# Two attention layers whose units run in pairs on both halves of PE's rows and columns, with the output rows begun by token half

## The chip, the cores and the metric

The kernel runs on one core of a Trainium2 chip. The metric is the device time of one execution in microseconds (us). Three executions before the change took 1319.76, 1322.01 and 1323.81 us; the median is 1322.01 us.

## The reference

Two transformer blocks run one after the other on one sequence of 256 tokens and 1024 features, all in float32. The first block has two layers. Each is a mixer (attention) with an output projection, and a SwiGLU feed-forward. The second block has a feed-forward, a mixer of short convolution and state-space scan, and another feed-forward. The change touches the two attentions of the first block and what follows them directly:

```
mixer_ab: q (8 heads x 64), three branches on the same heads
  compressed keys (15), selected keys, window keys, each gated; then 8 more heads with sinks
mixer_cd: 8 softmax heads (causal over 256 tokens), 8 "stick-breaking" heads
each softmax head:   s = q @ k.T * 0.125 + bias(distance);  p = softmax(s);  o = p @ v
y = concat(o) @ w_out          # 1024 x 1024, the output rows
x = x + gate * rms_norm(y, w)
```

With 256 tokens every selection takes all blocks, so selected and window attention are dense and causal.

## The kernel before

One program is written out by hand for five engines, each in its own function (`pe`, `act`, `dve`, `pool`, `sp`), and all walk the same list of weight chunks (`stream_plan`). A chunk is 1 MB; SP loads it into one of five `raw` buffers. A weight half (128x1024) is split in two: ACT writes the rounded part into `HI`, DVE the remainder into `LO` (L1281), in six slots (`HL`), and PE multiplies by both (three matmuls for one product). A modulation chunk is used by DVE alone, in one fused product and sum (L1271). Every engine calls the same planner (`Walk`): `weight` brings the stream up to a half, `catch_up(n, ahead)` goes further, and `spare(n)` takes up to n modulation halves only.

The attention is cut into **units**. A unit is one query tile (`qt`, 128 tokens) of one branch and of either four heads on 128 keys (qt 0) or two heads on 256 keys (qt 1); both are 128x512 scores, one PSUM bank. Heads 0 to 3 lie on partitions 0 to 63 of the query tiles `FMT`, heads 4 to 7 on 64 to 127 (`hs`), so a score matmul uses 64 of PE's rows. The values matmul uses all rows and 64 of PE's columns; its half is that of the output's partitions (`o_ap`). `AB` has 18 units (selected, window and sink branch, six each), `CD` has 6. The accumulators of the attention output lie in PSUM banks 0 to 3; four banks more are work banks, taken and given in turn (`Banks`).

A unit goes through the engines like this: `scores` (PE), `biased` (DVE: scale and bias in one pass, L1443, the row maximum in a second, L1449 or L1457, and its negation), `exps` (ACT, one exponential per head, with its sum), `scaled` (DVE: 1/sum, gate, product, L1432), `transposes` (PE, four 128x128, L585), `moved` (ACT, copy out of PSUM), `values` (PE). `attend` runs one unit per step on each engine; on PE a step is

```
scores(tag, i, *U_[i])
if i > 1:
    transposes(tag, i - 2)
banks.give(("s", tag, i))
walk.spare(spare)
if between:
    between(i)
if i > 2:
    values(tag, i - 3, *U_[i - 3])
```

`between` weaves other work into the steps: in the first attention the compressed branch (`cmp_keys`, `cmp_values`, `cmp_scores`, `cmp_turn`, `cmp_out`, on DVE also `cmp_windows`), in the second the stick-breaking heads (`two_stages`). Three score slots and three slots for transposed scores (`s_slot`, `p_slot`) hold the units in flight.

After the last unit, `out_parts` copies each accumulator bank as `HH` (ACT) and `HLo` (DVE, L1348), `linear_out` runs the 8 contraction tiles of the output rows (`rows`: 12 matmuls of 128x512 per tile, both token halves one after the other; before the first, PE waits for the last `HLo`), `add_normed` adds the result to `x`, and `modulate` prepares the input of the feed-forward.

## Time and profile before

| | us |
|---|---|
| median of the executions | 1322.01 |
| the profiled execution | 1324.44 |
| its span | 1322.6 |
| mean granted TensorE clock, share of full | 0.963 |
| first attention: first score matmul to the end of the last values | 112.2 to 204.3 |
| its output rows | 209.2 to 232.2 |
| second attention | 506.7 to 550.4 |
| its output rows | 553.6 to 577.3 |

Times count from the span's start. PE stands for TensorE's matmuls, DVE for VectorE, ACT for ScalarE. A float32 matmul or transpose is counted as two instructions where both operands are plain float32. The end of a matmul is modelled and overlaps the start of the next, so that in a row "x8" the distance to the next row's start is the time that counts.

### The profile page before, as it was taken

The page shows a single profiled execution, that of the slowest core. Times are in us where ns is not written, and L with a number is a line of the kernel's source. Part 1 is how long each engine was busy: PE and PEld are TensorE (multiplying, and loading weights), DVE is VectorE, ACT ScalarE, POOL GpSimd, SP SyncE. Part 2 cuts the span into 40 slices and gives each one's busy share as a digit, 9 for nine tenths or more (in the row PEclk, how much of TensorE's full clock was granted, in tenths as well). Part 3 has the DMA queues.
Part 4 walks back from the last instruction along what each step waited for, and adds up shares of the span by engine and source line. Part 5 has one row for each costly group of instructions (what it writes and reads, how often), then busy time and mean ns, then how long its engine had stood idle before and what let it go on. Part 6 is the DMA issues. An engine that isn't in the chain of part 4 may idle for free.

```text
span 1322.6 us, 20076 instructions
## 1 busy us (share of the span) xinstructions
PE 1210.4 (92%) x8504; PEld 1093.4 (83%) x8504; DVE 939.8 (71%) x1506; ACT 583.9 (44%) x952; POOL 74.4 (6%) x105
## 2 busy tenths in 40 slices
PE   0787988999999998889999999999999997999996
PEld 0776646899989797579999989999988986999995
DVE  5865574888977884558888868887764967665544
ACT  0442354544344544645444455444443254544442
POOL 0000000000000000008700000000000000000000
PEclk9997698999999997989999999999999999999998
DMA  9790404378898393036789844878951264565830
GB/s 377 288 377 24 192 1 161 139 305 318 264 333 311 126 393 119 32 111 226 284 318 241 340 183 176 304 289 231 370 204 68 97 134 153 182 241 217 205 128 32
DMA packets 40809, 280.83 MB, mean 212 GB/s; under 512 B 4736, under 2 KB 5264, under 8 KB 7952
## 3 DMA queue, kind: packets, MB, share of 16 engines
q1 hardware_dynamic: 37296, 269.27, 56.2%
q0 software_dynamic: 2416, 7.92, 1.9%
q10 hardware_dynamic: 1008, 2.37, 0.5%
q8 instruction: 66, 1.08, 0.3%
q14 instruction: 23, 0.19, 0.1%
HBM read 277.91 MB, written 1.10 MB: 211 GB/s over the span
## 4 chain that ended last, share of the span: by engine, by line
PE 72%; DVE 16%; ACT 5%; DMA 5%; issue 1%; SPq 0%; DVEq 0%; ACTq 0%
PE PS L401 71%; DVE LO L1281 5%; DMA raw<-WS 4%; DVE raw L1271 3%; ACT HI L894 1%; ACT SQ L894 1%; PE PS L585 1%; DMA SC<-scratch 1%; DVE TMP L1333 1%; DVE X L1382 1%; ACT SC L894 1%; DVE TMP L1361 1%; ACT NR L894 0%; DVE SC L1443 0%; ACT FB L894 0%
## 5 line engine op out<-in xcount | busy, mean ns | idle before, releaser
L401 PE MATMUL PS<-HH,HI 128*128 128x256 f32 x1748 | 498.4, 285 | 3.0 <-DVE LO L1281 3.0
L401 PE MATMUL PS<-HLo,HI 128*128 128x256 f32 x1748 | 495.1, 283 | 0.3 <-DVE HLo L1328 0.3
L401 PE MATMUL PS<-HH,LO 128*128 128x256 f32 x1748 | 494.2, 283 | 0.0
L1281 DVE TENSOR_TENSOR LO<-raw,HI 128x1024 fp32r<-128x1024 f32 x340 | 403.7, 1226 | 121.7 <-ACT HI L894 121.7
L894 ACT ACTIVATE HI<-raw 128x1024 fp32r<-128x1024 f32 x340 | 339.7, 1048 | 119.6 <-PE PS L401 69.4
L401 PEld LDWEIGHTS PS<-HH,HI 128*128 128x128 f32 x1748 | 334.9, 192 | 8.7 <-DVE LO L1281 4.9
L401 PEld LDWEIGHTS PS<-HH,LO 128*128 128x128 f32 x1748 | 334.8, 192 | 3.3 <-issue 0.5
L401 PEld LDWEIGHTS PS<-HLo,HI 128*128 128x128 f32 x1748 | 334.7, 192 | 1.4 <-DVE HLo L1328 1.2
L1271 DVE CUSTOM_DVE_ANT_0 raw<-raw,CB,SM 128x1024 f32<-128x1024 f32 x168 | 210.6, 1284 | 23.2 <-DMA raw<-WS 23.0
L401 PE MATMUL PS<-HI,HDH 128*128 128x512 f32 x352 | 140.2, 398 | 0.0
L401 PE MATMUL PS<-HI,HDL 128*128 128x512 f32 x352 | 139.5, 396 | 0.0
L401 PE MATMUL PS<-LO,HDH 128*128 128x512 f32 x352 | 138.9, 394 | 0.0
L894 ACT ACTIVATE HDH<-FB 128x256 fp32r<-128x256 f32 x88 | 36.8, 418 | 208.6 <-DVE FB L1404 208.6
L894 ACT ACTIVATE FB<-PS 128x256 f32<-128x256 f32 (+1 forms) x94 | 38.0, 404 | 127.9 <-PE PS L401 127.7
L894 ACT ACTIVATE SC<-PS 128x512 f32<-128x512 f32 (+3 forms) x65 | 36.6, 573 | 122.3 <-PE PS L401 63.6
L401 PE MATMUL PS<-RS,X 128*128 128x128 f32 x224 | 39.1, 333 | 46.9 <-DVE RS L1323 46.9
L401 PE MATMUL PS<-SC 128*64 128x256 f32 (+5 forms) x352 | 76.3, 395 | 4.3 <-DMA SC<-scratch 2.3
L401 PEld LDWEIGHTS PS<-HI,HDL 128*128 128x128 f32 x352 | 66.4, 189 | 15.9
L401 PEld LDWEIGHTS PS<-RS,X 128*128 128x128 f32 x224 | 36.0, 245 | 50.8 <-issue 30.3
L401 PEld LDWEIGHTS PS<-LO,HDH 128*128 128x128 f32 x352 | 66.5, 189 | 12.8
L401 PEld LDWEIGHTS PS<-HI,HDH 128*128 128x128 f32 x352 | 66.4, 189 | 12.4
L401 PE MATMUL PS<-HI,HH 128*128 128x512 f32 (+2 forms) x176 | 62.9, 357 | 13.9 <-DVE HLo L1348 9.1
(222 smaller groups left out, 1125.1 us busy)
## 6 DMA issues: line engine op xcount, KB each, us to landing
raw<-WS SPq DMA_DIRECT2D x255, 1024.0 KB, 5.5
SC<-scratch POOLq DMA_DIRECT2D x2, 1024.0 KB, 13.1
FB<-gates_out POOLq DMA_DIRECT2D x3, 512.0 KB, 5.1
SQ<-gates_out POOLq DMA_DIRECT2D x3, 512.0 KB, 9.8
X<-xT ACTq DMA_DIRECT2D x1, 1024.0 KB, 6.9
SC<-ssm POOLq DMA_DIRECT2D x2, 512.0 KB, 4.1
out<-TMP SPq DMA_DIRECT2D x2, 512.0 KB, 2.7
CB<-vecs SPq DMA_DIRECT2D x1, 512.0 KB, 6.5
```

What stands on the lines that cost most here:

```text
L401: return e.matmul(o, l, r, start=start, stop=stop, skip_group_check=True)
L585: x = e.transpose(ps[:, n * 128:(n + 1) * 128], s[:, n * 128:(n + 1) * 128], C("ident"))
L894: return e.activation(o, a, f, **k)
L1271: e.tensor_tensor_reduce(x, x, CB[:, :], 1.0, S("mb")[:, c:c + 1], O.mult, O.add, MV[:, c:c + 1]) \
L1281: e.tensor_tensor(LO[:, s % HL, :], raw_half(j, h), HI[:, s % HL, :].bitcast(fp32), O.subtract).then_inc(*D.up(("lo", s)))
L1333: e.tensor_scalar(TMP[:, k, :], turned(k), AV[:, k:k + 1], MV[:, sh + k:sh + k + 1], O.mult, O.add) \
L1361: e.tensor_tensor(gy[qt], acc_rows(qt), grow(tag), O.mult).then_inc(*D.up())
L1382: e.tensor_tensor(X[:, qt, :], X[:, qt, :], gy[qt], O.add).then_inc(*D.up(("x", tag, qt)))
```

## The change

Units go in pairs (one of heads 0 to 3, one of heads 4 to 7). PE issues the scores of both in turn, on rows 0 to 63 and 64 to 127, into two banks, and the values of both in turn, on columns 0 to 63 and 64 to 127. The units of two heads are put in the order h0 = 0, 4, 2, 6 so that neighbours form a pair. The compressed scores and outputs go in turn on the two halves as well. There are six score slots (two of them in `RS`) and four transposed ones. The factor 0.125 moves into the copy of the queries out of PSUM, and bias and maximum become one fused pass per head on DVE (`tensor_tensor_reduce`, the instruction form of L1271, with PSUM as a source). Step p of the first attention has, on PE, transposes of pair p-2, scores of pair p, compressed work, values of pair p-3; on DVE, the fused passes of pair p, scalings of pair p-1, up to two modulation halves. From step 6 on every engine also takes one more half of the stream, which here are halves of the output weights. The window sums of the compressed branch move ahead of the first pass. The output rows are issued by token half (`out_half`): four contraction tiles of the first half go between the last transposes and values of the first attention.

```diff
-        def s_slot(i):
-            return SC[:, 8704 + (i % 3) * 512:9216 + (i % 3) * 512]
+        def s_slot(tag, i):
+            if i % 6 in (3, 4):
+                return flat(RS[:, 2 * (i % 6) - 6:2 * (i % 6) - 4, :])
...
-        quads = [(0, 4, h0) for h0 in (0, 4)] + [(1, 2, h0) for h0 in (0, 2, 4, 6)]
+        quads = [(0, 4, h0) for h0 in (0, 4)] + [(1, 2, h0) for h0 in (0, 4, 2, 6)]
...
-            def scores(tag, i, q0, ktile, vcol, bh, b, gate, sink, last, qt, nh, h0):
+            def scores(tag, U_, p):
+                pair = (2 * p, 2 * p + 1)
+                ps = [take(("s", tag, i)) for i in pair]
...
                 for n in range(nh):
+                    for o, i in zip(ps, pair):
+                        q0, ktile, qt, h0 = [U_[i][x] for x in (0, 1, 8, 10)]
+                        hs = slice(h0 // 4 * 64, h0 // 4 * 64 + 64)
+                        x = mm(o[:, n * kw:(n + 1) * kw], FMT[hs, q0 + (h0 + n) % 4, qt * 128:qt * 128 + 128],
+                               FMT[hs, ktile, 0:kw], n == 0, True)
...
+            def out_half(name, ks, qt):
+                for k in ks:
+                    key = (name, k // 2)
+                    wt = weight(key, k % 2)
+                    w.wait_ge(*A.at(("hh", name, k)))
+                    w.wait_ge(*D.at(("hlo", name, k | 1 if qt == 0 and k > 3 else 3 if qt == 0 else 7)))
+                    rows(name, (HH, HLo), k, wt, k == 0, k == 7, [used(key, k % 2)] if qt else [], (qt,))
...
-            attend("ab", AB, 0, 18, 1, woven)
-            drain("ab", AB)
-            linear_out("abo")
+            for p in range(9):
+                if p > 1:
+                    transposes("ab", p - 2)
+                scores("ab", AB, p)
+                walk.spare(2)
+                for f in compressed.get(p, ()):
+                    f()
+                if p > 5:
+                    walk.catch_up(walk.unit - 1, 1)
+                if p > 2:
+                    values("ab", AB, p - 3)
+            transposes("ab", 7)
+            values("ab", AB, 6)
+            out_half("abo", (0, 1), 0)
+            transposes("ab", 8)
+            values("ab", AB, 7)
+            out_half("abo", (2, 3), 0)
+            values("ab", AB, 8)
+            out_half("abo", (4, 5), 0)
+            out_half("abo", (0, 1), 1)
+            out_half("abo", (6, 7), 0)
+            out_half("abo", range(2, 8), 1)
...
-            attend("cd", CD, 0, 6, 2, two_stages)
-            drain("cd", CD)
-            linear_out("cdo")
+            for i in range(6):
+                if 1 < i < 5:
+                    transposes("cd", i - 2)
+                if i < 3:
+                    scores("cd", CD, i)
+                walk.spare(2)
+                two_stages(i)
+                if i > 2:
+                    values("cd", CD, i - 3)
+            out_half("cdo", (0, 1, 2, 3, 4, 5), 0)
+            out_half("cdo", (0, 1), 1)
+            out_half("cdo", (6, 7), 0)
+            out_half("cdo", range(2, 8), 1)
...
             def biased(tag, i, q0, ktile, vcol, bh, b, gate, sink, last, qt, nh, h0):
...
-                e.scalar_tensor_tensor(s3, bank(("s", tag, i)).rearrange("p (h k) -> p h k", h=nh), 0.125,
-                                       BI[:, bh + h0:bh + h0 + nh, bo:bo + kw], O.mult, O.add) \
-                    .then_inc(*D.up(("free", ("s", tag, i))))
+                for n in range(nh):
+                    e.tensor_tensor_reduce(s3[:, n, :], bank(("s", tag, i))[:, n * kw:(n + 1) * kw],
+                                           BI[:, bh + h0 + n, bo:bo + kw], 1.0,
+                                           sk[:, n:n + 1] if sink else eps[:, 1:2], O.add, O.max, m[:, n:n + 1]) \
+                        .then_inc(*D.up(("free", ("s", tag, i))))
```

The rows of the two programs at three places. On **PE**, one step in the middle of the first attention (`SC` and `RS` hold scores, `TMP` and `SQ` the compressed branch). Before, with transposes, a compressed output, values of one unit and scores of one unit:

```order
L585 MATMUL PS<-CN,SC 128x128 x4
L401 MATMUL PS<-TMP,SQ 64x2x128 x2
L401 MATMUL PS<-SC 64x2x128 x2
L401 MATMUL PS<-SC 128x256 x2
L585 MATMUL PS<-CN,SC 128x128 x4
```

and of the change, from the transposes of one pair to those of the next:

```order
L599 MATMUL PS<-CN,RS 128x128 x4
L599 MATMUL PS<-CN,SC 128x128 x4
L406 MATMUL PS<-SC 128x256 x4
L406 MATMUL PS<-TMP,SQ 64x2x128 x4
L406 MATMUL PS<-SC 64x2x128 x4
```

The scores now stand behind the transposes of the same step, and four score and four values matmuls (two units) stand together. On **DVE**, one sink unit of two heads, before:

```order
L1443 SCALAR_TENSOR_TENSOR SC<-PS,SC 128x512
L1449 TENSOR_REDUCE SC<-SC 128x2
L1451 TENSOR_TENSOR SC<-SC,SM 128x2
L1453 TENSOR_TENSOR SC<-SM,SC 128x2
L1455 TENSOR_SCALAR SC<-SC 128x2
```

and of the change, with the half of the output weights that stands ahead of the pair:

```order
L1324 TENSOR_TENSOR LO<-raw,HI 128x1024
L1490 ISA RS,SC<-PS,SC,SM 128x256
L1490 ISA SC 128x1
L1490 ISA RS,SC<-PS,SC,SM 128x256
L1490 ISA SC 128x1
L1496 TENSOR_TENSOR SC<-SM,SC 128x2
L1498 TENSOR_SCALAR SC<-SC 128x2
```

Two passes over 512 elements and three small steps became one fused pass of 256 per head, each with a read of its accumulator, and two small steps. On **PE** at the end of the first attention, before:

```order
L401 MATMUL PS<-SC 64x2x128 x2
L585 MATMUL PS<-CN,SC 128x128 x4
L401 MATMUL PS<-SC 64x2x128 x4
L401 MATMUL PS<-HI,HH 128x512
L401 MATMUL PS<-LO,HH 128x512
L401 MATMUL PS<-HI,HLo 128x512
```

and of the change:

```order
L406 MATMUL PS<-HI,HLo 128x512
L599 MATMUL PS<-CN,RS 128x128 x4
L599 MATMUL PS<-CN,SC 128x128 x4
L406 MATMUL PS<-SC 64x2x128 x4
L406 MATMUL PS<-HI,HH 128x512
```

The last pair's transposes and the values of the pair before it now stand behind the first two tiles of the output rows, and two tiles more stand ahead of the last values.

## Rows read from the trace of the kernel before

**Rows 1.** The page, part 4: what the chain that ended last consists of.
```profile
PE 72%; DVE 16%; ACT 5%; DMA 5%; issue 1%; SPq 0%; DVEq 0%; ACTq 0%
```

**Rows 2.** By stretch: length, busy (count) of PE, PEld, DVE, ACT, POOL; clock; DMA share.
```profile
112.00:126.00 14.00, 6.98 (x58) 6.21 (x58) 10.86 (x25) 4.87 (x21) 1.45 (x2) 0.71 0.06 4
126.00:142.00 16.00, 15.94 (x117) 12.00 (x117) 6.29 (x15) 5.65 (x19) 0.00 (x0) 0.82 0.34 126
142.00:162.00 20.00, 19.94 (x64) 13.12 (x62) 11.66 (x38) 6.28 (x25) 0.00 (x0) 0.50 0.57 240
162.00:196.00 34.00, 30.08 (x149) 17.79 (x148) 24.62 (x82) 19.71 (x65) 0.00 (x0) 1.00 0.00 1
196.00:209.10 13.10, 6.70 (x20) 3.57 (x20) 4.89 (x13) 5.96 (x8) 0.00 (x0) 0.64 0.00 0
209.10:232.20 23.10, 23.04 (x93) 18.94 (x94) 13.64 (x12) 10.05 (x11) 0.00 (x0) 0.91 0.65 236
506.70:553.60 46.90, 34.67 (x192) 26.35 (x192) 27.19 (x58) 27.17 (x59) 0.54 (x1) 0.85 0.04 12
553.60:577.30 23.70, 23.70 (x97) 19.45 (x98) 10.92 (x10) 9.84 (x14) 0.00 (x0) 0.93 0.45 160
```

**Rows 3.** PE's order of time: start us, busy us, group, [idle before <-releaser].
```profile
121.46 1.09 PE L585 MATMUL PS<-CN,SC 128*128 128x128 f32 x4 [6.99 <-DVE SC L1432]
...
134.74 1.96 PE L401 MATMUL PS<-raw,SQ 128*15 128x64 f32 x32
...
182.62 0.66 PE L585 MATMUL PS<-CN,SC 128*128 128x128 f32 x4
183.21 2.13 PE L401 MATMUL PS<-SC 128*64 128x256 f32 x8
...
197.56 1.12 PE L585 MATMUL PS<-CN,SC 128*128 128x128 f32 x4 [4.20 <-DVE SC L1432]
...
209.16 0.77 PE L401 MATMUL PS<-HI,HH 128*128 128x512 f32 x1 [4.90 <-DVE LO L1281]
```

**Rows 4.** PE's order of time, second attention: stick values; start of the output rows.
```profile
526.50 0.88 PE L401 MATMUL PS<-SC 128*64 128x256 f32 x8
527.20 0.87 PE L401 MATMUL PS<-SQ,SC 128*64 128x256 f32 x8
...
553.60 0.50 PE L401 MATMUL PS<-HI,HH 128*128 128x512 f32 x1 [3.21 <-DVE HLo L1348]
```

**Rows 5.** PE alone in two narrow stretches: stick scores; output rows.
```profile
508.38:510.74 2.36, 2.36 (x17) 0.58 0.05 7
214.00:232.00 18.00, 18.00 (x81) 1.00 0.68 249
```

**Rows 6.** DVE's order of time in the first attention.
```profile
114.75 1.93 DVE L1494 TENSOR_TENSOR SQ<-SC,SM 64x480 f32<-64x480 f32 x2
...
120.44 0.88 DVE L1432 TENSOR_SCALAR SC<-SC 128x128 f32<-128x128 f32 x4
...
168.15 0.62 DVE L1432 TENSOR_SCALAR SC<-SC 128x256 f32<-128x256 f32 x2
...
185.84 0.68 DVE L1443 SCALAR_TENSOR_TENSOR SC<-PS,SC 128x512 f32<-128x512 f32 x1
...
187.28 0.16 DVE L1451 TENSOR_TENSOR SC<-SC,SM 128x2 f32<-128x2 f32 x1
...
204.94 1.29 DVE L1348 TENSOR_TENSOR HLo<-PS,HH 128x512 fp32r<-128x512 f32 x2 [6.50 <-ACT HH L894]
```

**Rows 7.** DVE's costliest groups on the page: its two instructions for the stream.
```profile
L1281 DVE TENSOR_TENSOR LO<-raw,HI 128x1024 fp32r<-128x1024 f32 x340 | 403.7, 1226 | 121.7 <-ACT HI L894 121.7
...
L1271 DVE CUSTOM_DVE_ANT_0 raw<-raw,CB,SM 128x1024 f32<-128x1024 f32 x168 | 210.6, 1284 | 23.2 <-DMA raw<-WS 23.0
```

**Rows 8.** ACT's order of time: the first halves of the output weights.
```profile
206.70 5.79 ACT L894 ACTIVATE HI<-raw 128x1024 fp32r<-128x1024 f32 x6
```

**Rows 9.** The feed-forward that follows, columns as in rows 2.
```profile
241.00:435.00 194.00, 190.69 (x1339) 178.25 (x1340) 157.96 (x270) 85.41 (x123) 1.46 (x2) 0.99 0.76 279
```

More of the change, by code:

```diff
@@ L492, in values_only, with rows @@
                 banks.give((key, 0))
-            def rows(name, acts, k, wt, first, last, done):
-                for qt in range(2):
+            def rows(name, acts, k, wt, first, last, done, qts=(0, 1)):
+                for qt in qts:
                     a = [x[:, k, qt * 128:qt * 128 + 128] for x in acts]
@@ L504, in rows, with linear_out @@
                             i.then_inc(*P.up(("acc", name, 2 * qt + h)))
[L505 to L509 removed]
+                if done:
+                    i.then_inc(*P.up(("acc", name, 3), *done))
+            def linear_out(name, ks):
                 for k in ks:
@@ L592, in pv, with values @@
                 return mm(o, l, r, first, stop)
-            def values(tag, i, q0, ktile, vcol, bh, b, gate, sink, last, qt, nh, h0):
-                g, nk, pt = h0 // 4, qt + 1, p_slot(i)
-                w.wait_ge(*A.at(("free", ("t", tag, i))))
-                p4 = pt.rearrange("p (h k n) -> p k h n", h=nh, k=nk)
-                for n in range(0, nh, 2):
-                    for kt in range(nk):
-                        pr = (h0 + n) % 4
+            def values(tag, U_, p):
+                pair = (2 * p, 2 * p + 1)
+                for i in pair:
+                    w.wait_ge(*A.at(("free", ("t", tag, i))))
+                nh, nk = U_[2 * p][9], U_[2 * p][8] + 1
+                steps = [(n, kt) for n in range(0, nh, 2) for kt in range(nk)]
+                for n, kt in steps:
+                    for i in pair:
+                        vcol, b, last, qt, h0 = [U_[i][x] for x in (2, 4, 7, 8, 10)]
+                        g, pr = h0 // 4, (h0 + n) % 4
+                        p4 = p_slot(tag, i).rearrange("p (h k n) -> p k h n", h=nh, k=nk)
@@ L601, in values @@
                         x = pv(b, pr, g, o_ap(b, pr, g, qt), VT[:, kt, vcol + g * 64:vcol + g * 64 + 64],
                                p4[:, kt, n:n + 2, :], last and kt == nk - 1)
-                x.then_inc(*P.up(("v", tag, i)))
-            def attend(tag, U_, a, b, spare, between=None):
-                for i in range(a, b):
-                    scores(tag, i, *U_[i])
-                    if i > 1:
-                        transposes(tag, i - 2)
-                    banks.give(("s", tag, i))
-                    walk.spare(spare)
-                    if between:
-                        between(i)
-                    if i > 2:
-                        values(tag, i - 3, *U_[i - 3])
@@ L1169, in two_stages @@
                     f(g)
-            attend("cd", CD, 0, 6, 2, two_stages)
-            moved("cd", 4)
-            moved("cd", 5)
+            for n in range(6):
+                for i in (2 * n - 4, 2 * n - 3):
+                    if 1 < n < 5:
+                        moved("cd", i)
+                for i in (2 * n, 2 * n + 1):
+                    if n < 3:
+                        exps("cd", i, *CD[i])
+                high(walk.spare(2))
+                two_stages(n)
             w.wait_ge(*P.at(("v", "cd", 5)))
@@ L1650, in dve @@
             gate("f1", 64, 1.0, S("nw")[:, 40:48])
-            attend("cd", CD, 0, 6, 2, two_stages)
-            scaled("cd", 4, *CD[4])
-            scaled("cd", 5, *CD[5])
+            for n in range(6):
+                for i in (2 * n, 2 * n + 1):
+                    if n < 3:
+                        biased("cd", i, *CD[i])
+                for i in (2 * n - 2, 2 * n - 1):
+                    if 0 < n < 4:
+                        scaled("cd", i, *CD[i])
+                low(walk.spare(2))
+                two_stages(n)
             for i in range(4):
```

227 lines of the change are left out of this document (113 added, 114 removed).

## Prediction

> **What bounds the kernel now.** I read the chain that ended last first: 72% of it is PE [rows 1]. So the question is where PE is not full. The table by stretch says so for the two attentions and what follows them [rows 2]: PE is busy 15.94 of 16 us and 19.94 of 20 us from 126 to 162, but 6.98 of 14 before, 30.08 of 34 from 162 to 196, 6.70 of 13.1 up to the output rows, and 34.67 of 46.9 in the second attention. The output rows are full again (23.04 of 23.1), and so is the feed-forward (190.69 of 194, [rows 9]): what an attention ends earlier passes through to the end, and nothing after it takes it back. PE's order of time names the three large waits of the first attention [rows 3]: 6.99 us for the first scaling, 4.20 for the last one, 4.90 for the first `LO` of the output weights; the second has 3.21 for `HLo` [rows 4]. The same table holds the second cause, the granted clock: 0.71, 0.82, 0.50, 1.00, 0.64 in the five stretches of the first attention. 0.50 is the lower of PE's two levels (1.2 GHz), 1.00 the upper (2.4). Weighted by length the mean is 0.78, so 45% of the 97 us ran at the lower level. It had fallen before the wait of 6.99 ended and again in the low stretch from 142, where PE was dense.
>
> **Pairs on PE.** The scores of one unit and the values of another, 512 streamed columns each, take 2.13 us together at the upper level (183.21, [rows 3]), about 1.03 and 1.0; in pairs one behind the other it would be 4.1. That the halves can overlap is in the trace: the stick values alternate between the column halves and start a group every 0.70 us (526.50 to 527.20, [rows 4]), where their 2 x (256 + 128) columns would need 1.5 at 1.0 for 512; the stick scores on row halves took 2.36 us for 1536 columns at a clock of 0.58 [rows 5], 5.2 by the same price. So I take a pair of scores as 1.03 and a pair of values as 1.0, the price of one unit. The other end is no overlap (a rival). Transposes stay: a start every 0.59 us per unit (182.62 to 183.21), 1.1 at the lower level.
>
> **The fused pass on DVE.** Before, a unit costs a pass of 0.68 (starts 0.72 apart), a maximum of about the same, and in a sink unit three small steps of 0.16, 0.19 apart [rows 6]. The fused form on 1024 elements is 1.284 against 1.226 for a plain product of two tensors [rows 7]. Between starts I take 1.07 for 1024 elements, 0.14 fixed and 0.08 for the accumulator: 0.40 for 256, 0.27 for 128. A unit is then 0.96 (two heads, with 0.16 for the negation), 1.24 (four), 1.15 and 1.43 with a sink, against about 1.3 and 1.9: a small gain on two heads, none on four. The ends: 0.14 less per pass if the fixed part overlaps, twice the streaming part if it runs at half rate. I take the middle because the nearest row is the same form.
>
> **The first attention, step by step** (upper level first). First passes start at 113.3 as before. The windows (2 x 1.93, the row of 114.75, [rows 6]) now stand ahead. To the first scaled pair: 3.9 + passes of four units 2 x 1.24 + 2 x 0.96 + one scaling 1.2 = 9.5, so PE's first transposes start at 122.8 against 121.46: a loss of 1.3.
>
> DVE's work up to the scaling of unit 15: windows 3.9; passes of 18 units 8 x 0.96 + 4 x 1.24 + 4 x 1.15 + 2 x 1.43 = 20.1; scalings, of two heads 0.54 + two small steps = 0.93, of four 0.80 + 0.39 = 1.19 (168.15 and 120.44, [rows 6]), 10 x 0.93 + 6 x 1.19 = 16.4; compressed steps 3.6 (some 18 small ones at 0.2); two modulation halves 2.4 and two `LO` 2.3 [rows 7]. Sum 48.7.
>
> The change adds a wait. Scores of pair p now stand on PE behind the transposes of pair p-2, which need DVE's last scaling; DVE's next pass waits for those scores. So per step DVE stands idle for the second transposes 0.59, the scores 1.03 and some 0.1 between engines: 1.7, in steps 2 to 8, 7 x 1.7 = 11.9. Compressed values (a start 1.9 after the last, 134.74, [rows 3]; two in step 2) add 1.9. The halves of the stream and the compressed steps that DVE does behind its scalings hide 3.5 of it. That is 10.3, and unit 15 is scaled at 113.3 + 48.7 + 10.3 = 172.3.
>
> From there 14.3: `LO` 1.15, last scalings 1.9, `HLo` of two banks 1.2 (204.94, [rows 6]), two half tiles of output rows 2.8, transposes 1.2, values 1.0, two half tiles 2.8, values 1.0, and 1.2 of waits between. All values are done at 186.6 at the upper level. The wait of 4.20 is filled by the half tiles. That of 4.90 goes: the six `HI` that were made at 206.70 in 5.79 us [rows 8] are partly made at steps 6 to 8.
>
> The clock: I keep the share of before, four of the seven waits of 1.7 at the lower level (3.2, 4 x 1.5 = 6.0), one compressed group (1.6) and one group of the tail (1.6): 9.2. Values end at **195.8** against 204.3.
>
> Output rows: 0.227 us for a matmul of 128x512 (81 in 18.00, [rows 5]), six in a half tile, 1.36, up to 1.41. Twelve half tiles are left, 16.6, and 1.1 to 1.9 for slots of weights that come free late (`HI` and `LO` of 6 and 7 wait for a slot whose second token half comes after the fifth tile). The rows end at 195.8 + 18.2 = **214.0** against 232.2: -18.2.
>
> The second attention: on PE three pairs of scores and values save at most 6 x 1.03 = 6.2, DVE six passes of 0.36 = 2.2; PE was idle 12.2 of 46.9 us [rows 2] and the stick chain, which sets much of the order, is not shorter. Of 8.4 I take 2.9. The rows start 1.9 after it instead of 3.2 (two `HLo` banks instead of four), -1.3, and lose 1.1 in the late slots: **-3.1**.
>
> Elsewhere nothing: the factor 0.125 rides in a copy that ACT makes anyway, the constant is one small store on POOL ahead of all, SP's loads keep their order and DMA is at 0.57 or less in both attentions [rows 2]. Sum -21.3. The profiled execution took 1324.44; its changed twin would take about 1303, and against the median, 2.4 less, **1301**.
>
> **Rivals.**
> - *The clock stays up in the first attention and mostly in the second.* Against: it starts with the same wait. For: PE then alternates more evenly with DVE. Gives 9.2 more in the first, 4.9 in the second: 1287.
> - *Pairs don't overlap* (the change doesn't do what it says). Scores cost 1.03 more in seven waits, 7.2, and values 2.6 in the tail: -8.4 in the first, some 0 in the second: 1313.6. Against: [rows 4, 5].
> - *The fused pass runs at half rate*, 0.67 and 0.41: 10 x 0.54 + 6 x 0.56 = 8.8, less 2.4 in the steps where PE's compressed work ends last, so -11.8 in the first and -1.2 in the second: 1309. Against: the row of 1.284 beside 1.226 [rows 7], whose sources both lie in SBUF. The Trainium skill, "Vector Engine (DVE) Microarchitecture Reference", section on points easy to get wrong, says that the related two-source form with accumulator halves its throughput for two sources in SBUF that are not bf16; by that rule the time would be 1309, and the trace disagrees for the long form.
> - *Slower: the lower level throughout.* PE now waits in every step, and if the clock stays at 0.5 from the first wait to the output rows, seven waits cost 10.5 more, compressed groups 3.2, the tail 8.5: values at 208.8, rows end at 227.3 (-4.9), while the second attention and its first rows, doubled in PE's 34.7 less what is low already, lose 9.7: 1322 + 4.8 = 1327. It decides where the granted clock of both stretches is below about 0.6. Against: the stretch of 162 to 196, with PE at 88% and waits in it, ran at 1.00 [rows 2].
>
> **How the numbers follow.** Forecast 0.70, clock up 0.12, no overlap 0.06, half rate 0.08, low clock throughout 0.04. The range 1286 to 1315 takes in all but the last, and leaves about 0.15 for sums off by more. A measurement of this kernel tells 0.3%, 4 us, from no change. Faster by more: 0.92 (all cases but the last, less 0.04 for several misses together); same 0.04; slower 0.04.
>
> **What would show it.** In the profile after: values of the first attention end near 196, rows near 214; eight score matmuls of two units in about 1.0 us at the upper level; fused passes 0.40 apart; DVE idle some 1.7 per step, released by PE's matmuls; no wait of 4.9 for `LO`; the feed-forward still 194 long. Wrong would be: pairs at 2 us, passes at 0.67, waits of 3 or more at a clock of 0.5 in most steps, or a stall of more than 2 us in the output rows.

## The result, and the profile after

| | before | changed |
|---|---|---|
| median of the executions, us | 1322.91 (4) | 1301.29 (4; 1298.90 to 1306.79) |
| ratio to before, with 95% interval | | 0.9842 [0.9801, 0.9884] |
| the profiled execution, us | 1324.44 | 1303.10 |
| its span, us | 1322.6 | 1301.0 |
| first attention: first score matmul | 112.2 | 110.6 |
| end of its last values | 204.3 | 191.6 |
| its output rows: end | 233.0 | 209.8 |
| first transposes of the next stage | 241.3 | 218.7 |
| second attention: first scores to output rows | 46.9 | 44.3 |
| its output rows | 23.5 | 24.9 |
| from their end to the next stage | 9.9 | 10.5 |

The change was measured once more: 1299.96 us over five executions, ratio 0.9836 [0.9818, 0.9854]. Two single executions of 3998 and 6555 us, of a variant and of the kernel before, stand far from all others; they don't move the medians, and the ratios are formed without them.

The next stage starts 22.6 us earlier (218.7 for 241.3), more than the 21.6 us by which the span is shorter. Not all of it is the change: the first score matmul starts at 110.58 instead of 112.23, and ahead of it the change edits only a factor in a copy and one stored constant. In the other profiles of the changed kernel and its variants that start lies between 108.9 and 112.0, so these 1.65 us are within the spread from one execution to the next. From the first score matmul to the end of the last values it was 92.0 us and is now 81.0. The second attention gains 2.5 us up to its rows and gives 2.1 of it back in the rows and behind them.

The stretches of the changed kernel, columns as in [rows 2]:

```profile
112.00:126.00 14.00, 8.59 (x59) 6.52 (x56) 10.39 (x45) 6.48 (x28) 1.32 (x2) 0.68 0.12 36
126.00:142.00 16.00, 11.90 (x134) 9.99 (x133) 10.98 (x53) 8.04 (x31) 0.00 (x0) 0.82 0.68 277
142.00:162.00 20.00, 16.67 (x122) 10.52 (x122) 15.45 (x82) 13.34 (x46) 0.00 (x0) 0.86 0.23 97
162.00:186.00 24.00, 16.79 (x78) 10.48 (x76) 14.50 (x57) 10.49 (x30) 0.00 (x0) 0.72 0.13 45
186.00:196.00 10.00, 9.37 (x46) 6.41 (x47) 4.79 (x5) 5.84 (x8) 0.00 (x0) 1.00 0.55 208
192.00:209.70 17.70, 16.59 (x72) 13.36 (x73) 8.18 (x8) 8.58 (x10) 0.00 (x0) 1.00 0.48 171
484.10:529.20 45.10, 29.71 (x192) 22.95 (x192) 24.66 (x83) 26.21 (x60) 0.54 (x1) 0.81 0.06 13
529.20:554.00 24.80, 23.63 (x96) 19.04 (x97) 10.85 (x11) 10.41 (x12) 0.00 (x0) 0.93 0.30 103
```

In 112 to 162 PE is no longer dense (it was 15.94 of 16 and 19.94 of 20 in two of these, [rows 2]), and DVE does more in the same time: from 126 to 162 26.43 us of work against 17.95. The clock is 0.68 to 0.86 up to 186, with no long stretch at 0.50; over 112 to 192 it is 0.79, in the second run of the change 0.74. The output rows are dense again.

PE's order of time, the same columns as in [rows 3]:

```profile
121.43 2.22 PE L599 MATMUL PS<-CN,SC 128*128 128x128 f32 x8 [1.32 <-DVE SC L1469]
123.58 2.08 PE L406 MATMUL PS<-SC 64*128 64x256 f32 x8
...
160.63 1.13 PE L406 MATMUL PS<-SC 64*128 64x256 f32 x8 [0.49 <-ACT TMP L930]
...
166.42 0.63 PE L599 MATMUL PS<-CN,SC 128*128 128x128 f32 x4 [2.63 <-DVE SC L1467]
...
173.84 0.63 PE L599 MATMUL PS<-CN,SC 128*128 128x128 f32 x4 [1.93 <-DVE SC L1467]
...
179.39 0.76 PE L406 MATMUL PS<-HI,HH 128*128 128x512 f32 x1 [1.79 <-DVE HLo L1391]
...
191.86 0.47 PE L406 MATMUL PS<-HI,HH 128*128 128x512 f32 x1 [0.28 <-DVE HLo L1391]
...
198.69 0.50 PE L406 MATMUL PS<-HI,HH 128*128 128x512 f32 x1 [1.11 <-DVE LO L1324]
...
218.69 3.67 PE L406 MATMUL PS<-RS,X 128*128 128x128 f32 x18 [3.33 <-DVE RS L1366]
```

The first transposes start at 121.43, where they started before (121.46). Counted from the first score matmul they come later, 10.85 us behind it instead of 9.23. A pair's scores take 1.13 us at the upper level (160.63) and 2.08 at the lower (123.58). The last transposes (184.64) no longer wait, where they had waited 4.20, and the wait of 4.90 is gone. Waits of about 2 stand ahead of earlier transposes (166.42, 173.84), and one of 1.79 for `HLo` is new (179.39). The output rows behind the last values run from 191.86 to 209.76, 17.9 us, with one stall of 1.11.

DVE's order of time, steps 0 and 2 to 7:

```profile
111.50 3.92 DVE L1526 TENSOR_TENSOR SQ<-SC,SM 64x480 f32<-64x480 f32 x4
...
125.69 0.48 DVE L1490 CUSTOM_DVE_ANT_0 RS<-PS,SC,eps 128x256 f32<-128x256 f32 x1 [3.21 <-PE PS L406]
...
132.43 0.35 DVE L1490 CUSTOM_DVE_ANT_0 SC<-PS,SC,eps 128x128 f32<-128x128 f32 x1 [2.80 <-PE PS L406]
...
132.70 0.35 DVE L1490 CUSTOM_DVE_ANT_0 SC<-PS,SC,eps 128x128 f32<-128x128 f32 x1
...
141.76 0.48 DVE L1490 CUSTOM_DVE_ANT_0 SC<-PS,SC,eps 128x256 f32<-128x256 f32 x1 [1.73 <-PE PS L406]
...
148.78 0.48 DVE L1490 CUSTOM_DVE_ANT_0 RS<-PS,SC,eps 128x256 f32<-128x256 f32 x1 [0.65 <-PE PS L406]
...
154.55 0.35 DVE L1490 CUSTOM_DVE_ANT_0 SC<-PS,SC,SM 128x128 f32<-128x128 f32 x1 [0.90 <-PE PS L406]
...
161.46 1.23 DVE L1324 TENSOR_TENSOR LO<-raw,HI 128x1024 fp32r<-128x1024 f32 x1 [2.03 <-ACT HI L930]
```

The windows ran from 111.50, 0.92 us behind the first score matmul. Fused passes start 0.27 apart for 128 elements (132.43, 132.70). At 125.69, 132.43, 141.76, 148.78 and 154.55 (and at 170.29 below) DVE waits for the scores that stand on PE behind the transposes, 11.0 us in all. Such waits are not new. In the kernel before, DVE waited for scores 24.3 us in sum over the same attention, at the longest here:

```profile
128.14 0.69 DVE L1443 SCALAR_TENSOR_TENSOR SC<-PS,SC 128x512 f32<-128x512 f32 x1 [4.31 <-PE PS L401]
...
154.22 0.69 DVE L1443 SCALAR_TENSOR_TENSOR SC<-PS,SC 128x512 f32<-128x512 f32 x1 [4.51 <-PE PS L401]
```

What is new is the reason: then PE was mostly dense, now its order puts the scores behind transposes that need DVE. 161.46 waits for `HI` of the output weights.

DVE's order of time, step 8 and the end of the output rows:

```profile
170.29 0.48 DVE L1490 CUSTOM_DVE_ANT_0 RS<-PS,SC,SM 128x256 f32<-128x256 f32 x1 [1.68 <-PE PS L406]
...
204.31 2.53 DVE L1324 TENSOR_TENSOR LO<-raw,HI 128x1024 fp32r<-128x1024 f32 x2 [4.38 <-ACT HI L930]
207.03 2.53 DVE L1324 TENSOR_TENSOR LO<-raw,HI 128x1024 fp32r<-128x1024 f32 x2 [0.20 <-ACT HI L930]
209.48 1.88 DVE L1413 TENSOR_TENSOR TMP<-PS,FB 128x512 f32<-128x512 f32 x3
...
213.51 2.48 DVE L1418 SCALAR_TENSOR_TENSOR X<-TMP,NR,X 128x1024 f32<-128x1024 f32 x2
```

### The profile page after: what moved, and what is told of

Its sections match the earlier page's. It is cut to its first block, busy times and chain, and to the rows that moved or that the text cites. A ratio compares the mean times of both kernels' runs of the same rounds, so it can differ in the third digit from the quotient of the medians.

```text
span 1301.0 us, 20185 instructions
## 1 busy us (share of the span) xinstructions
PE 1180.5 (91%) x8504; PEld 1074.6 (83%) x8504; DVE 931.4 (72%) x1600; ACT 581.6 (45%) x952; POOL 74.4 (6%) x106
## 3 DMA queue, kind: packets, MB, share of 16 engines
q8 instruction: 66, 1.08, 0.3%
## 4 chain that ended last, share of the span: by engine, by line
PE 70%; DVE 17%; ACT 6%; DMA 4%; issue 1%; SPq 0%; DVEq 0%; ACTq 0%
PE PS L406 69%; DVE LO L1324 5%; DVE raw L1314 3%; DMA raw<-WS 3%; ACT HI L930 2%; ACT SQ L930 1%; DMA SC<-scratch 1%; DVE SC L1490 1%; ACT SC L930 1%; DVE SC L1475 1%; DVE X L1425 1%; DVE TMP L1404 1%; PE PS L599 1%; ACT NR L930 0%; ACT FB L930 0%
## 5 line engine op out<-in xcount | busy, mean ns | idle before, releaser
L1324 DVE TENSOR_TENSOR LO<-raw,HI 128x1024 fp32r<-128x1024 f32 x340 | 403.8, 1225 | 132.2 <-ACT HI L930 131.7
L1314 DVE CUSTOM_DVE_ANT_0 raw<-raw,CB,SM 128x1024 f32<-128x1024 f32 x168 | 210.3, 1283 | 24.6 <-DMA raw<-WS 24.5
L406 PEld LDWEIGHTS PS<-HI,HDL 128*128 128x128 f32 x352 | 66.4, 189 | 15.9
L406 PEld LDWEIGHTS PS<-HI,HDH 128*128 128x128 f32 x352 | 66.4, 189 | 12.4
L1447 DVE TENSOR_TENSOR FB<-FB,PS 128x256 f32<-128x256 f32 x88 | 36.5, 415 | 51.9 <-ACT FB L930 51.8
```

What stands on the lines that cost most here:

```text
L406: return e.matmul(o, l, r, start=start, stop=stop, skip_group_check=True)
L1314: e.tensor_tensor_reduce(x, x, CB[:, :], 1.0, S("mb")[:, c:c + 1], O.mult, O.add, MV[:, c:c + 1]) \
L1324: e.tensor_tensor(LO[:, s % HL, :], raw_half(j, h), HI[:, s % HL, :].bitcast(fp32), O.subtract).then_inc(*D.up(("lo", s)))
L1447: e.tensor_tensor(HF[:, j % 2, :], SIL[:, j % 2, :], bank((key, 0))[:, 256:512], O.mult) \
```

## The experiments

All ratios are to executions of the kernel before that were taken beside those of the run. The milestones are from PE's order of time in each trace. "Same half", "both" and "and half product" were taken beside "change, again", and are compared with it.

| run | median us | ratio [95%] | first scores start | last values end | rows end | next stage | second attention to rows, rows |
|---|---|---|---|---|---|---|---|
| change | 1301.29 | 0.9842 [0.9801, 0.9884] | 110.6 | 191.6 | 209.8 | 218.7 | 44.3, 24.9 |
| change, again | 1299.96 | 0.9836 [0.9818, 0.9854] | 110.5 | 192.1 | 210.2 | 219.2 | 42.6, 24.9 |
| serial issue | 1296.51 | 0.9814 [0.9796, 0.9833] | 110.5 | 188.7 | 206.8 | 215.8 | 42.7, 23.3 |
| two passes | 1311.12 | 0.9925 [0.9909, 0.9940] | 110.8 | 200.1 | 218.3 | 227.2 | 47.4, 23.3 |
| rows late | 1298.57 | 0.9842 [0.9800, 0.9883] | 110.7 | 180.1 | 208.1 | 216.3 | 43.4, 24.9 |
| and weights late | 1303.73 | 0.9863 [0.9838, 0.9888] | 109.6 | 178.8 | 210.3 | 218.6 | 44.2, 24.9 |
| filled waits | 1304.61 | 0.9865 [0.9824, 0.9905] | 110.6 | 192.8 | 210.9 | 219.8 | 44.4, 24.9 |
| other order | 1292.36 | 0.9782 [0.9755, 0.9809] | 108.9 | 186.2 | 202.9 | 211.9 | 43.4, 23.5 |
| windows back | 1297.50 | 0.9823 [0.9789, 0.9858] | 112.0 | 190.8 | 208.9 | 217.8 | 44.2, 24.9 |
| scores first | 1292.33 | 0.9788 [0.9760, 0.9817] | 109.4 | 182.0 | 200.2 | 209.1 | 44.4, 24.9 |
| same half | 1306.88 | 0.9894 [0.9876, 0.9912] | 110.5 | 193.2 | 211.3 | 220.3 | 49.3, 24.9 |
| both | 1287.61 | 0.9743 [0.9729, 0.9756] | 109.4 | 180.4 | 197.2 | 206.1 | 43.4, 23.5 |
| and half product | 1284.57 | 0.9720 [0.9699, 0.9740] | 110.9 | 180.7 | 197.5 | 205.9 | 44.3, 23.4 |

How far two profiles of one kernel differ is seen in the stretch from the next stage to the second attention, which no run edits: it took 266.2 us in the change, 265.0 in its second run and 262.4 to 265.6 in the others. So a difference of 2 to 3 us in one profile, or of 3 between medians, is not a result by itself; the columns show where a difference sits. The start of the first scores, ahead of which the variants edit nothing either, differs by 3.1 us among them, so times of the first attention are best compared after subtracting it.

### Serial issue

```diff
-                for n in range(nh):
-                    for o, i in zip(ps, pair):
+                for o, i in zip(ps, pair):
+                    for n in range(nh):
...
-                for n, kt in steps:
-                    for i in pair:
+                for i in pair:
+                    for n, kt in steps:
```

> The changed kernel, but the scores of a pair are issued one unit after the other, and the values too. Theory of the prediction (the halves of PE overlap in a pair, and the seven waits of DVE for scores hold that time): scores of a pair go from about 1.0 to about 2.0 us at the upper level, 7.2 us more in the waits and 2 to 4 in the tail; output rows of the first attention end 9 to 13 us later than in the changed kernel (209.8), whole time near 1311 to 1314. Rival (the gain comes from order and DVE, PE's matmuls stand beside DVE's work): less than 3 us more, time below 1305.

The slower time of the theory did not come: the median is 1296.51. That is the rival's number, but not for the rival's reason. PE's order of time in that run has the scores of a pair of two-head units and of a pair of four-head units, each time all of one unit and then all of the other:

```profile
152.71 1.71 PE L406 MATMUL PS<-SC 64*128 64x128 f32 x16
...
159.98 1.14 PE L406 MATMUL PS<-SC 64*128 64x256 f32 x8 [0.49 <-ACT TMP L930]
```

and in the change, in turn:

```profile
153.35 1.16 PE L406 MATMUL PS<-SC 64*128 64x128 f32 x16
```

The pair of two heads takes 1.14 us, as in the change (1.13). In the single records the second unit's first matmul starts 0.02 us behind the first unit's (160.00, 159.98), ahead of the rest of that unit. A pair of values takes 1.09 us (162.07), in turn 1.08. So for the pairs of two heads, two thirds of all, the edit did not take the sharing away. For the pair of four heads it took half of it: the second unit starts 0.55 us late (153.26), with the fifth of the first unit's eight instructions (two for each matmul), and the next row starts 1.64 us after the first instead of 1.09. There are four such pairs, so the run could test only about 2 us of the theory. Its ratio is lower (0.9814), but the interval overlaps those of both runs of the change, and 1.8 of its 7.8 us in span lie in the stretch that nothing edits. The second run of the change, 1299.96, is too near to the first to say that this run is lower by more than the spread. Whether issuing one after the other is a little better stays open.

### Same half

```diff
+        plain = [(0, 4, h0) for h0 in (0, 4)] + [(1, 2, h0) for h0 in (0, 2, 4, 6)]
...
-            return [(q0, ktile, vcol, bh, b, gate, sink, last) + u for u in quads]
+            return [(q0, ktile, vcol, bh, b, gate, sink, last) + u for u in (quads if sink else plain)]
```

> The changed kernel, but units of two heads of the first two branches and of the second attention are paired within one half (heads 0-1 with 2-3, 4-5 with 6-7), so six of the twelve pairs cannot share the array. Theory (what saves PE's time is that neighbours lie on different halves, whatever the order of issue within the pair, as the run with serial issue showed 1.14 us for a pair of scores): those pairs take about 2.0 us for scores and 2.0 for values at the upper level, DVE's waits in steps 2, 4 and 5 grow by 1 to 2 us each, the second attention by 1 to 2: whole time 3 to 7 us above the changed kernel of the same call. Rival (adjacent matmuls on the same half overlap as well): pairs stay near 1.1 us, less than 1 us.

Measured: 6.9 us above the change (1306.88 against 1299.96). PE's order of time, a pair of scores and one of values on one half, and a pair of scores on both halves in the sink branch:

```profile
152.40 1.99 PE L407 MATMUL PS<-SC 64*128 64x256 f32 x8
...
155.29 1.94 PE L407 MATMUL PS<-SC 128*64 128x256 f32 x8
...
165.85 1.14 PE L407 MATMUL PS<-SC 64*128 64x256 f32 x8 [0.49 <-ACT TMP L931]
```

1.99 and 1.94 against 1.14. The price of the pair was right, and the sharing is what makes it: the units are the same and only their neighbours differ. The 6.9 us are its worth for six of the twelve pairs. DVE's waits in steps 2 to 5 were 4.07, 4.74, 2.58 and 2.27, in the second run of the change 3.21, 2.94, 1.73 and 1.60: 4.2 us more. But the last values ended only 1.1 later; the rest, 6.7 us, is in the second attention (49.3 against 42.6), where the forecast had put 1 to 2. The later steps of the first attention ran with shorter waits than in that run of the change (0.74 against 2.14 in step 8, and the output rows started at the upper level), and the first run of the change took 44.3 us in the second attention, so the split between the two attentions is less sure than the sum.

### Two passes

```diff
-                for n in range(nh):
-                    e.tensor_tensor_reduce(s3[:, n, :], bank(("s", tag, i))[:, n * kw:(n + 1) * kw],
...
+                e.tensor_tensor(s3, bank(("s", tag, i)).rearrange("p (h k) -> p h k", h=nh),
+                                BI[:, bh + h0:bh + h0 + nh, bo:bo + kw], O.add) \
+                    .then_inc(*D.up(("free", ("s", tag, i))))
+                w.wait_ge(*D.now())
+                e.tensor_reduce(m, s3, X_AX, O.max).then_inc(*D.up())
...
```

In a unit with a sink the maximum with the sink is a third step again.

> The changed kernel, but bias and maximum in two passes over 512 elements again. Theory (the fused pass lies on the path in the first attention): a unit of two heads costs 0.4 to 0.6 us more, one of four 0.2 to 0.3; 16 units on the chain give 6 to 8 us, the second attention about 1; time near 1309. Rival (DVE waits for PE in each step, so the pass is covered): less than 2 us more, time below 1304.

Measured 1311.12, some 10 us above the change. DVE's order of time in step 2:

```profile
127.44 0.69 DVE L1489 TENSOR_TENSOR RS<-PS,SC 128x512 f32<-128x512 f32 x1 [3.21 <-PE PS L406]
128.17 0.69 DVE L1493 TENSOR_REDUCE SC<-RS 128x2 f32<-128x512 f32 x1
...
130.48 0.16 DVE L1469 RECIPROCAL SC<-SC 128x2 f32<-128x2 f32 x1
```

A pair of two-head units takes 3.04 us (127.44 to 130.48), in the change 2.01; a pair of four-head units 3.04 against 2.56. In the sink branch it is 3.82 against 2.40 for two heads and 3.82 against 2.95 for four. Over the nine pairs that makes 4 x 1.03 + 2 x 0.48 + 2 x 1.42 + 0.87 = 8.8, and the last values end 8.5 later, 8.3 counted from the first scores. DVE's waits did not shrink to cover it (13.3 us in steps 2 to 8, in the change 13.4), so the fused pass is on the path almost in full. The second attention, 3.1 longer, had been expected to lose 1.

### Rows late, and weights late

```diff
             values("ab", AB, 6)
-            out_half("abo", (0, 1), 0)
             transposes("ab", 8)
             values("ab", AB, 7)
-            out_half("abo", (2, 3), 0)
             values("ab", AB, 8)
...
+            w.wait_ge(*D.at(("hlo", "abo", 7)))
+            linear_out("abo", range(8))
```

> The changed kernel, but in the first attention all output rows stand behind the last values, both token halves of a tile together; the early halves of weights stay. Theory of the prediction (the half tiles fill waits): the four half tiles that moved, 5.6 us at the upper level, come back, output rows end 4 to 6 us later than 209.8. Rival, worked out from the trace of the changed kernel: transposes 8 could start near 178, values end near 183 and HLo near 185, then 16 half tiles of 1.36 give 207 to 209, so no loss (within 1.5 us of 209.8).

The theory of the prediction fell: rows end at 208.1, 1.7 earlier than with them woven in. PE's order of time:

```profile
176.24 1.12 PE L599 MATMUL PS<-CN,RS 128*128 128x128 f32 x4
...
178.13 1.95 PE L406 MATMUL PS<-SC 128*64 128x256 f32 x16
184.56 0.60 PE L406 MATMUL PS<-HI,HH 128*128 128x512 f32 x1 [4.48 <-DVE HLo L1387]
```

The last transposes run at 176.24 instead of 184.64 and the last values end at 180.1 instead of 191.6. After them PE waits 4.48 us for `HLo`, and that wait costs no more than the half tiles had cost in front of the values: all four in the change stood ahead of work that others needed, and the first two ran at the lower level (179.39 to 184.64, 0.44 us per matmul). The run also gives up the order by token half, and with it the stall of 1.11 us in the rows and 0.7 behind them. Without these two, woven and late rows differ by about 1 us.

The second run also takes away the halves of the output weights in steps 6 to 8 (`catch_up` on three engines).

> As the run with the output rows late, and also without the three halves of output weights made in steps 6 to 8. Theory of the prediction (the wait of 4.9 us for the first LO comes back): 3 to 5 us later than the run with rows late alone. Rival: the three LO and the waits for their HI stand on DVE's chain, 0.9 in step 7 and 1.5 in step 8, and give back about half: 0 to 2 us later.

Last values 1.3 us earlier, output rows end 2.3 later; counted from the first scores, which start 1.1 earlier, that is 0.2 and 3.4. PE's wait for `HLo` behind the last values is 7.65 us (186.45), with the early weights 4.48. The medians differ by 5.2, the ratios by 0.0021 (2.8 us) with intervals that overlap. So the early weights are worth about 3 us: less than the 4.90 of [rows 3], in the lower part of the theory's range if the start is subtracted and just above the rival's if not. The run does not decide between the two.

### Filled waits

```diff
+                    if tag == "ab" and i % 2 == 0:
+                        for _ in range(10):
+                            mm(ps[:, 0:256], zb[:, 0:128], zb, True, True)
                     w.wait_ge(*D.at(("p", tag, i)))
```

> The changed kernel with ten matmuls of 128x256 on zeros ahead of PE's wait for the first transposes of each pair in the first attention (about 1.1 us at the upper level, into the bank that the transposes then write). Theory (the granted clock falls where PE waits between groups, and what is lower than 1.00 costs time in the waits of DVE): the mean granted clock from 112 to the output rows rises from 0.80 to over 0.9 and values end 2 to 5 us earlier. Rival (the level does not follow these waits, the added matmuls only delay the transposes where PE was on time): clock within 0.05 of 0.80, 0 to 5 us later.

By stretch, the change:

```profile
112.00:192.00 80.00, 59.32 (x409) 40.64 (x406) 55.42 (x238) 42.66 (x140) 1.32 (x2) 0.79 0.28 107
```

and with the waits filled:

```profile
112.00:192.00 80.00, 64.51 (x494) 46.24 (x492) 54.55 (x237) 42.41 (x139) 1.33 (x2) 0.87 0.27 102
```

The granted clock was 0.87 where the two runs of the change have 0.79 and 0.74 (one profile each), and the last values ended 1.2 us later, not earlier. So with its waits filled PE was granted more, though not the 0.9 of the theory. What it gave was spent in part by the fillers, which delayed transposes that were ready: at 144.82 they took 2.11 us ahead of transposes that in the change had not waited (145.19). The clock half of the theory held in part, the time did not; the rival's time came, but not its clock.

### Windows back

```diff
-            cmp_windows(0)
-            cmp_windows(1)
             for p in range(9):
                 for i in (2 * p, 2 * p + 1):
                     biased("ab", i, *AB[i])
+                    if p == 0:
+                        cmp_windows(i)
```

> The changed kernel with the window sums back between the passes of the first two units. Theory of the prediction (windows ahead cost what they take at the start): nothing to gain, since both stand before the first scaling in either order; within 1 us. Rival (their place decides when PE gets its first long work and so the clock): the granted clock from 112 to 142 changes by over 0.05 and the time by 2 us or more, in either direction.

Last values 0.8 us earlier, ratio 0.9823 [0.9789, 0.9858]: no difference that can be told. The granted clock from 112 to 142 was 0.77, in the change 0.75 and 0.76 in its two runs. The rival fell, and the theory's "nothing to gain" stands. The first transposes come 11.18 us behind the first score matmul with the windows back and 10.85 with them ahead, so their place is worth 0.3 us. The last values end 78.7 us behind it, in the change 81.0 and 81.6; this lies in steps 3 and 8 and the tail, and no run says whether it is more than spread.

### Scores first

```diff
+                scores("ab", AB, p)
                 if p > 1:
                     transposes("ab", p - 2)
-                scores("ab", AB, p)
```

> The changed kernel with the scores of pair p ahead of the transposes of pair p-2 on PE. Theory of the prediction (DVE waits in each step for transposes and scores, 1.7 us): DVE's idle time before its fused passes, 10.9 us in steps 2 to 8 of the changed kernel, falls by more than half, values end 4 to 8 us earlier. Rival (transposes then come later and with them the values and slots; compressed scores wait for the banks of the passes): less than 1.5 us of change.

The last values end 9.6 us earlier, 8.4 counted from the first scores, a little more than the 4 to 8 that were expected. The median is 8 to 9 us lower, by the ratios 6 to 7. All that is left of DVE's idle time in steps 2 to 7:

```profile
127.76 0.35 DVE L1490 CUSTOM_DVE_ANT_0 SC<-PS,SC,eps 128x128 f32<-128x128 f32 x1 [2.62 <-PE PS L406]
...
143.17 0.48 DVE L1490 CUSTOM_DVE_ANT_0 RS<-PS,SC,eps 128x256 f32<-128x256 f32 x1 [1.51 <-PE PS L406]
...
154.88 1.22 DVE L1324 TENSOR_TENSOR LO<-raw,HI 128x1024 fp32r<-128x1024 f32 x1 [2.03 <-ACT HI L930]
```

6.2 us with the wait for `HI`, in the change 11.3 over the same steps (3.21, 2.80, 1.73, 0.65, 0.90, 2.03), and in step 8 0.37 against 2.04. That is 6.8 us less of waiting. The wait that comes from the order on PE was real and was avoidable.

### Other order, both, and half product

```diff
+            out_parts("abo", 0)
+            out_parts("abo", 1)
             scaled("ab", 16, *AB[16])
             scaled("ab", 17, *AB[17])
-            out_parts("abo", 0)
-            out_parts("abo", 1)
...
             out_half("abo", (0, 1), 1)
+            out_half("abo", (2, 3), 1)
             out_half("abo", (6, 7), 0)
-            out_half("abo", range(2, 8), 1)
+            out_half("abo", range(4, 8), 1)
...
```

The second attention has the same edit of `out_half`.

> The changed kernel, with the second token half of tiles 2 and 3 ahead of the first half of 6 and 7 in both output rows, and HLo of the first two banks ahead of the scaling of the last pair. Theory: the stalls of 1.11 us for late slots go in both attentions, and PE's wait of 1.79 for HLo too: output rows of the first attention 2 to 3.5 us earlier, of the second 1 us, time near 1297. Rival (the stall moves to the next slot, and the last transposes come later by the 1.3 us that HLo takes): less than 1 us in sum.

PE's order of time holds every wait from 173 to the end of the rows:

```profile
174.73 0.77 PE L406 MATMUL PS<-HI,HH 128*128 128x512 f32 x1 [0.41 <-DVE SC L1469]
...
183.53 0.50 PE L406 MATMUL PS<-HI,HH 128*128 128x512 f32 x1 [0.35 <-DVE LO L1326]
...
186.50 0.47 PE L406 MATMUL PS<-HI,HH 128*128 128x512 f32 x1 [0.29 <-DVE HLo L1393]
```

The wait of 1.79 at the first row is 0.41, the stall of 1.11 is gone, and in the second attention the rows are back at 23.5. (Serial issue and two passes have 23.3 there with the stall still in them: they had no matmul of these rows at the lower level behind the first, the others six to eight.) That is 2.5 us and 1.4, as forecast; the median fell by more, 9 us (the profiled span 12.2), of which 1.7 is time ahead of the first scores that the edit does not touch (DVE's wait for the scores of step 2 ends at 124.0 instead of 125.7), about 1.9 lies in the stretch that no run edits, and about 1 is a shorter wait in step 8 (0.74 against 1.68). So the mechanism is shown and the last part of its size is not.

This run also bears on rows late. In this order the woven rows end 94.0 us behind the first scores, with rows late 97.3 (one profile each): weaving half tiles in seems to pay once `HLo` no longer comes too late for them.

> Scores first, and the other order of the half tiles with HLo ahead of the last scalings, together. Theory (they take away different waits: 13 us of DVE's idle time in the steps, and the stalls of slots and HLo behind them): the savings of 9 and 9 add up to 12 to 17 below the changed kernel of this call, near 1285. Rival (both end in the same wait of the tail): under 3 below the better of the two, near 1290.

12.4 us below the second run of the change, 14 below the first: they add, and the rival fell.

The last run splits `add_normed`: on DVE the products of the first two banks, and on ACT their squares, stand ahead of the last three weight halves.

```diff
-            linear_out("abo", range(2, 8))
-            add_normed("f0", "abo")
+            linear_out("abo", range(2, 5))
+            products("f0", "abo", (0, 1))
+            linear_out("abo", range(5, 8))
+            add_normed("f0", "abo", (2, 3))
```

> As the run with both, and the product and sum of squares of the first token half are issued on DVE and ACT ahead of the last weight halves, since their accumulation ends 5.6 us before the output rows do. Theory (after the change DVE's first product starts 0.28 us before the rows end, it was 1.77 before, because LO of the next stage stands ahead of it): the stretch from the end of the rows to the next stage falls from 8.9 to about 7.5 us in the first attention and from 10.5 to about 9.2 in the second, 2 to 3 us in all. Rival (LO of the next stage then comes too late for its first matmuls): no gain.

DVE's order of time at the end of the rows (they end at 197.5):

```profile
191.62 0.69 DVE L1421 TENSOR_TENSOR TMP<-PS,FB 128x512 f32<-128x512 f32 x1 [1.09 <-PE PS L406]
193.08 0.69 DVE L1421 TENSOR_TENSOR TMP<-PS,FB 128x512 f32<-128x512 f32 x1 [0.77 <-ACT SQ L932]
194.54 3.50 DVE L1332 TENSOR_TENSOR LO<-raw,HI 128x1024 fp32r<-128x1024 f32 x3 [0.77 <-ACT HI L932]
197.95 1.28 DVE L1421 TENSOR_TENSOR TMP<-PS,FB 128x512 f32<-128x512 f32 x2
```

From the end of the rows to the next stage 8.5 instead of 8.9 us, and 10.0 instead of 10.5 in the second attention: 1.0 in all, where 2 to 3 were expected. The products of the first half do run early (191.62), but three `LO` still stand ahead of those of the second half, which start 0.48 after the rows ended. Median 1284.57, ratio 0.9720 [0.9699, 0.9740], the lowest of all; its interval meets that of the run before.

## Why the prediction was right, and where it was not

The total was 1301 against 1301.29 and 1299.96. That it is so close is luck in part: terms were wrong in both directions, and 1.65 us of the profiled gain lie ahead of the first attention.

- **What bounds.** Held. Time saved in the first attention went through the feed-forward: 22.6 us earlier at its start, 21.6 at the end.
- **Pairs on PE.** The price held (1.13 and 1.08 against 1.03 and 1.0), and the same-half run shows that the sharing is the cause, worth 7 us for six of the twelve pairs. Issue in turn is not needed for pairs of two heads (1.14 in serial issue); for pairs of four it saves 0.55 us each. So the serial run hardly tests the rival "pairs don't overlap"; the same-half run does, and the rival fell.
- **The fused pass.** Held to the hundredth: 0.40 and 0.27 between starts (132.43, 132.70 for the short form), 0.96 for a plain unit of two heads expected and 1.00 found. The rival of half rate fell: 0.48 us for 256 elements, and 0.41 from one start to the next. Of the rule in the Trainium skill ("Vector Engine (DVE) Microarchitecture Reference", points easy to get wrong), on a form with two sources in SBUF, this trace shows no halving. The fused pass has one source in PSUM, so the rule does not speak of it; L1314 with both in SBUF takes 1.283 us for 1024 elements as before [rows 7]; and L1418, a `scalar_tensor_tensor` without an accumulator whose two float32 sources both lie in SBUF, takes 1.24 (2.48 for two), against 1.23 for the plain two-source pass of L1324. The same form with its accumulator in use occurs in no run. The pass is on the path almost in full, worth some 10 us. The prediction had called it a small gain, though its own unit prices (about 1.3 and 1.9 before, 0.96 to 1.43 after) make 7 us over 18 units.
- **First transposes, 1.3 us lost.** The sum held and its starting point did not. From the first score matmul they come 1.6 us later than before (10.85, 9.23), because the passes of four units now stand ahead of the first scaling; from the windows' start to the end of the first scaling it was 9.8 us, forecast 9.5. That they still start at 121.43 and not at 122.8 comes from the 1.65 us ahead of the attention, which no term of the forecast holds.
- **The waits of 1.7 per step.** The mechanism was right and it is the change's own loss: scores first takes it away. The size: 17.9 us forecast (10.3, and 7.6 for the lower level), 13.4 measured up to 176, with 2.4 of them for `HI` and not for PE. The step that failed is "four of seven at the lower level": scores ran at the lower level only in steps 2, 4 and 8, and in steps 5 and 6 compressed steps covered all but 0.65 and 0.90. DVE's own work was mis-sized the other way, 49.7 us where the sum had 48.7. Unit 15 was scaled at 174.5, forecast 179.9 with the low clock.
- **The tail.** From the scaling of unit 15 (174.5) to the last values 17.1 us, forecast 15.9 with the low clock; the new part is the wait of 1.79 for `HLo` behind the last scalings, which the sum held as 1.2 of waits.
- **"The wait of 4.20 is filled by the half tiles; that of 4.90 goes".** Both waits went, but neither was worth its length. Rows late lose nothing, and weights late about 3 us. The working treated idle PE as free room, while the half tiles moved in front of transposes and values that were nearly ready, and waited for `HLo` themselves.
- **Output rows.** From the last values to their end 18.2 forecast, 18.2 measured (191.57 to 209.76), with the stall of 1.11 as forecast. The end before was read as 232.2; the last output matmul ends at 233.0, which makes the gain of this part 0.8 larger than the text had it.
- **Behind the rows.** Missed: 0.7 us in each attention. `LO` of the next stage stands ahead of the first product on DVE and its slots come free later by token half (207.03, then 209.48, 0.28 before the rows end; before, 1.77).
- **The second attention.** -3.1 forecast, -0.4 measured: up to the rows -2.5 where the terms gave -4.2, in the rows +1.4 (forecast +1.1), behind them +0.7 (not forecast). The term of 2.9 was a share chosen between 0 and 8.4, and the second run of the change had 42.6 us to the rows instead of 44.3, so its size is known to about 2 us only.

So up to the next stage 4.4 more than forecast (1.65 ahead of the first scores, 0.8 from the end that was misread, 2.5 from the steps, less 0.7 lost behind the rows), the second attention 2.7 less, and 0.8 and 0.7 lost in the stretches between and behind, which have no edit: 21.6 against 21.3.

## What to carry to other kernels

When a pass is fused or two units share the array, look at what the new order makes an engine wait for: putting the scores behind the transposes of the same step cost 6 to 9 us, beside the 21.6 that were gained. Idle time at the end of a stage isn't worth its length until an experiment has moved work out of it again; here filling a wait of 4.2 us gave nothing as long as the work that filled it had a late input of its own. Before you read a gain off two profiles, look at a point ahead of every edit: here it had moved by 1.65 us on its own. When rows are issued by halves, check in which order buffer slots come free and what stands ahead of the first consumer of the finished half.

## What the runs showed that was not expected

- Score matmuls of two units on different row halves ran beside each other when all of one unit were issued before the other, if the unit had two heads: 1.14 us for the pair in serial issue, 1.13 in turn, 1.99 when both lay on the same half. The second unit's first matmul started ahead of matmuls that were issued before it (160.00, with the first unit's second at 160.28). With four heads per unit it started only 0.55 us after the first, and the pair took 1.64 instead of 1.09.
- The granted clock was 0.87 instead of 0.79 and 0.74 when PE's waits were filled with matmuls on zeros, and the time did not fall.
- The feed-forward and projections between the attentions, identical in all kernels, took 262.4 to 266.2 us in the profiles, and the first score matmul started at 108.9 to 112.2, so a single profile of this kernel is no measure of 1 or 2 us.
